# One order of work on five queues: gate, memory score and context row steps placed anew, and one query tile projected in plain fp32

## The reference, cut to what matters

```python
def memory_attention(q, mem_n, w_memkv):       # 4 heads of 64
    k, v = jnp.split(mem_n @ w_memkv, 2, axis=-1)
    s = jnp.einsum('bthd,bnhd->bhtn', q, k) * (MEM_HEAD_DIM ** -0.5)
    p = jax.nn.softmax(s, axis=-1)
    return jnp.einsum('bhtn,bnhd->bthd', p, v)

# first_block, per layer: q_mem and gate are columns of the same projection of h
branch = jnp.concatenate([mix, mem_o], axis=-1) * jax.nn.silu(gate)
x = x + branch @ w_out[i]
```

```python
def blk(qs):                                    # differential attention, 128 queries at a time
    s1 = jnp.einsum('bqhd,bkhd->bhqk', a, k1) * scale
    s2 = jnp.einsum('bqhd,bkhd->bhqk', b, k2) * scale
    w = jax.nn.softmax(s1, axis=-1) - lam * jax.nn.softmax(s2, axis=-1)
    return jnp.einsum('bhqk,bkhe->bqhe', w, v)

h  = _rms(x, g_pre) * (1.0 + scale) + shift
hc = _rms(xc, g_pre) * (1.0 + mod_c[1]) + mod_c[0]          # the context rows
y = jnp.concatenate([a_out * silu(na_g), b_out * silu(df_g), c_out * silu(cv_g)], -1) @ w_out
x_new = x + gate * _rms(y, g_post)
```

## Time and profile before

| | before |
|---|---|
| median of 3 runs | 1653.34 us (1653.30 to 1657.56) |
| the profiled execution | 1653.44 us |
| its span | 1651.6 us |
| PE busy | 1597.0 us, 97% of the span |
| DVE, ACT busy | 979.8 us (59%), 667.6 us (40%) |
| mean granted TensorE clock | 0.991 |

### The profile page before, as it was taken

How to read it: one execution, slowest core, us unless ns; L and a number is a source line. 1 busy time by engine, 2 the same in 40 slices (tenths; PEclk the granted TensorE clock), 3 DMA queues, 4 the chain that set the end, 5 groups by cost and what they waited for, 6 DMA issues and landing times.

```text
span 1651.6 us, 22948 instructions
## 1 busy us (share of the span) xinstructions
PE 1597.0 (97%) x8870; PEld 1277.7 (77%) x8870; DVE 979.8 (59%) x1803; ACT 667.6 (40%) x1323; POOL 140.7 (9%) x192
## 2 busy tenths in 40 slices
PE   7999999899999999999999999989999999999898
PEld 6977877687878878878888888865656887788676
DVE  1356454456556655665447787565665467876674
ACT  3365443424323323263313435244554325433653
POOL 4132100000000000002000110000112001000001
PEclk9999999899999999999999999999999999999899
DMA  8221244334654764462223111221003134213100
GB/s 289 81 77 50 103 153 117 80 82 121 190 158 120 155 185 139 148 151 68 92 96 109 56 54 40 92 93 58 1 26 96 48 107 140 58 39 128 52 14 39
DMA packets 171252, 161.36 MB, mean 98 GB/s; under 512 B 40374, under 2 KB 154280, under 8 KB 171112
## 3 DMA queue, kind: packets, MB, share of 16 engines
q1 hardware_dynamic: 151944, 126.97, 26.1%
q10 hardware_dynamic: 16928, 25.27, 4.7%
q0 software_dynamic: 2272, 7.64, 1.4%
HBM read 149.80 MB, written 11.18 MB: 97 GB/s over the span
## 4 chain that ended last, share of the span: by engine, by line
PE 83%; DVE 10%; ACT 4%; issue 2%; DMA 0%; POOL 0%; ACTq 0%; SPq 0%; POOLq 0%; DVEq 0%
PE psum L2596 46%; PE psum L2567 10%; PE psum L2630 7%; PE psum L3139 5%; PE psum L2621 4%; PE psum L3137 2%; PE psum L2775 2%; PE psum L2687 2%; PE psum L2730 2%; DVE arena L1999 1%; PE psum L2669 1%; PE psum L3010 1%; DVE arena L1969 1%; DVE wring_r L2076 1%; DVE arena L2133 1%
## 5 line engine op out<-in xcount | busy, mean ns | idle before, releaser
L2596 PE MATMUL psum<-hT_r,wring_r 128*128 128x512 f32 x1696 | 575.2, 393 | 3.6 <-ACT branch L1745 1.1
L2596 PEld LDWEIGHTS psum<-hT_r,wring_r 128*128 128x128 f32 x1696 | 319.3, 188 | 79.0 <-issue 10.0
L2596 PE MATMUL psum<-arena_r,wring_r 128*128 128x256 f32 (+1 forms) x1360 | 359.1, 333 | 0.7 <-ACT branch L1564 0.5
L1564 ACT ACTIVATE arena<-psum 128x512 f32<-128x512 f32 (+6 forms) x256 | 149.8, 611 | 416.0 <-PE psum L2596 244.2
L2596 PEld LDWEIGHTS psum<-arena_r,wring_r 128*128 128x128 f32 x1360 | 218.3, 190 | 26.2 <-issue 1.8
L2567 PE MATMUL psum<-arena 128*128 128x96 f32 (+9 forms) x1460 | 220.8, 365 | 16.9 <-ACT branch L1745 7.1
L2596 PE MATMUL psum<-arena_r 128*128 128x512 f32 (+1 forms) x720 | 224.5, 350 | 0.0
L2567 PEld LDWEIGHTS psum<-arena 128*128 128x128 f32 (+5 forms) x1460 | 160.8, 189 | 64.7 <-issue 31.9
L2596 PE MATMUL psum<-hT_r,arena_r 128*128 128x512 f32 x448 | 177.8, 397 | 1.8 <-DVE wring_r L2076 1.0
L2630 PE MATMUL psum<-ident,arena 128*128 128x128 f32 (+3 forms) x1104 | 145.9, 277 | 17.4 <-DMA arena<-in_c_ctx 7.4
L2630 PEld LDWEIGHTS psum<-ident,arena 128*128 128x128 f32 (+3 forms) x1104 | 125.2, 142 | 39.6 <-issue 14.6
(11 more groups left out here) (237 smaller groups left out, 1967.8 us busy)
## 6 DMA issues: line engine op xcount, KB each, us to landing
wring<-in_w_in_b SPq DMA_DIRECT2D x54, 512.0 KB, 5.9
arena<-in_w_mod ACTq DMA_DIRECT2D x16, 1536.0 KB, 8.3
wring<-in_w_in SPq DMA_DIRECT2D x16, 1536.0 KB, 6.9
wring<-in_w_out SPq DMA_DIRECT2D x8, 2048.0 KB, 8.4
wring<-in_w_in_a SPq DMA_DIRECT2D x5, 1536.0 KB, 6.6
arena<-x_dram SPq DMA_DIRECT2D x3, 2048.0 KB, 14.6
wring<-in_w_in SPq DMA_DIRECT2D x6, 1024.0 KB, 5.7
arena<-ebias_dram SPq DMA_DIRECT2D x144, 32.0 KB, 1.8
```

What stands on the lines that cost most here:

```text
L1564: return nc.scalar.activation(out, in_, ACT.Copy, scale=scale)
L2596: ins_ = nc.tensor.matmul(b[0:hi.shape[2], 0:width], w[:, k], v[:, k], start=k + p == 0, stop=(k, p) == (KT - 1, 2))
```

## The change

It does five things. In A, `mS` is cut in two steps of four banks, with `gate` 6 between them and `gate` 7 behind. In B, `gate` 4 goes ahead of `qm`, and `mS` follows `qm` directly. `hcT` of layer 1 moves from behind the last `doT` of layer 0 to a place ahead of `dPV` of the last but one item, so ahead of the last `dT` too. In layer 1, `nv` goes ahead of `nq`. And in layer 1's differential stage the first query tile is projected in plain fp32 (its own split steps go away), and the eight quarters of the output weights are split at items 8 to 11, two each, instead of items 4 to 8.

```diff
--- before.py
+++ after.py
@@ -36,7 +36,7 @@
-YO_SPLITS = {4: ((0, 0), (0, 1)), 5: ((0, 3),), 6: ((0, 2), (1, 0)), 7: ((1, 1), (1, 3)), 8: ((1, 2),)}
+YO_SPLITS = {8: ((0, 0), (0, 1)), 9: ((0, 3), (0, 2)), 10: ((1, 0), (1, 1)), 11: ((1, 3), (1, 2))}
@@ -169,9 +169,9 @@
     add("v" * 6, "AoT")
-    add("a" * 8, "mS", "A")
-    add("a", "gate", "A", 6)
-    add("a", "gate", "A", 7)
+    for part in range(2):
+        add("a" * 4, "mS", "A", part)
+        add("a", "gate", "A", 6 + part)
     add("av" * 4, "mT", "A")
@@ -198,11 +198,10 @@
-    for i in range(4):
+    for i in range(5):
         add("a", "gate", "B", i)
     add("av", "qm", "B")
-    add("a", "gate", "B", 4)
-    add("a" * 8, "mS", "B")
+    add("a" * 8, "mS", "B", 0)
     for g in range(2):
         add("aav", "Bproj", 0, g)
@@ -251,8 +250,11 @@
         add("av" * 3, "nvF", l)
-        add(lat_ctx * 3, "nq", l)
+        if l == 0:
+            add(lat_ctx * 3, "nq", l)
         add("aaaavv", "nv", l)
+        if l:
+            add(lat_ctx * 3, "nq", l)
         neighbourhood(add, l)
+def mem_jobs(key):
+
+    return range(8) if key[1] == "B" else range(4 * key[2], 4 * key[2] + 4)
@@ -497,7 +504,8 @@
-            rows = [(tiles[i - 1], 1)] if h == 1 and i else [(t, 0)] if n == 5 or (h == DH - 1 and i) else []
+            rows = [(tiles[i - 1], 1)] if h == 1 and i else [(t, 0)] if h == DH - 1 and i else []
+            rows = [row for row in rows if row[0] != tiles[0]]
@@ -523,9 +531,11 @@
             if todo:
                 project()
+            if n == len(items) and l == 0:
+                add("vvvv", "hcT", 1)
             if h == 0 and i:
                 add("v", "doT", l, tiles[i - 1])
-                if l:
+                if l and i > 1:
                     add("", "yb", tiles[i - 1], 1)
@@ -537,9 +547,7 @@
     add("v", "doT", l, last)
-    if l == 0:
-        add("vvvv", "hcT", 1)
-    else:
+    if l:
         add("", "yx", l, before)
...
@@ -2084,6 +2092,7 @@
                     dve.wait_ge(yo_w_hi, yo_ws.index((half, q)) + 1)
+                    read_by_pe(dve, ("yo", 1, 0, half, 1))
                     cut = slice(2 * q, 2 * q + 2)
...
@@ -3119,7 +3130,7 @@
                     if turned_last:
                         pe.wait_ge(last_hi, 1)
-                    elif l:
+                    elif l and t:
                         pe.wait_ge(yo_x_lo, yo_xs.index((t, piece)) + 1)
@@ -3128,14 +3139,14 @@
-                    for k in yo_rows(t, piece) if l and not turned_last else ():
+                    for k in yo_rows(t, piece) if l and t and not turned_last else ():
                         cut = slice(t * P, (t + 1) * P)
                         x_hi, x_lo, w_hi, w_lo = row_hi[t % 2][:, k], branch_r[:, k, cut], yo_hi[half][:, k], yo_lo[half][:, k]
-                        if t == 0:
+                        if t == 1:
                             pe.wait_ge(yo_w_lo, yo_ws.index((half, k // 2)) + 1)
                         for p, (v, m) in enumerate(((x_hi, w_hi), (x_lo, w_hi), (x_hi, w_lo))):
                             ins_ = nc.tensor.matmul(b, v, m, start=k + p == 0, stop=(k, p) == (5, 2))
-                    for k in yo_rows(t, piece) if l == 0 else ():
+                    for k in yo_rows(t, piece) if l == 0 or t == 0 else ():
                         ins_ = nc.tensor.matmul(b, src[:, k, tt * P:(tt + 1) * P], w[:, k], start=k == 0, stop=k == 5)
```

More of the change, by code:

```diff
@@ L932, in hybrid_stack_kernel @@
         before_mem = split_at[("Bproj", 1, 0), 0]
-        split_starts = [("wout", "A"), ("wout", "B"), ("hcT", 1)]
+        split_starts = [("wout", "A"), ("wout", "B"), ("doT", 0, TT - 1)]
         split_bounds = [sum(split_jobs(key) for key, _ in steps[:order_of[start]]) for start in split_starts]
@@ L1749, in _ @@
                     ph = "AB".index(key[1])
-                    for i in range(8):
-                        b = bank(key, i)
+                    for j_, i in enumerate(mem_jobs(key)):
+                        b = bank(key, j_)
                         act.wait_ge(mem_negmax, 8 * ph + i + 1)
@@ L2200, in _ @@
                     ph = "AB".index(key[1])
+                    jobs = mem_jobs(key)
                     def mem_normalise(i):
-                        evacuated(dve, key, i)
+                        evacuated(dve, key, i - jobs[0])
                         chained(nc.vector.reciprocal(m_rec[:, ph, i], m_sum[:, ph, i]))
@@ L2206, in mem_normalise @@
                             m_rec[:, ph, i].unsqueeze(2).to_broadcast([P, 2, NMEM])).then_inc(mem_probs, 1)
-                    for i in range(8):
-                        b = full(dve, key, i)
+                    for i in jobs:
+                        b = full(dve, key, i - jobs[0])
                         chained(nc.vector.reduce_max(m_max[:, ph, i], b[:, :].rearrange("p (h m) -> p h m", h=2), AX_X))
                         scaled(m_neg[:, ph, i], m_max[:, ph, i], -mem_scale).then_inc(mem_negmax, 1)
-                        if i:
+                        if i > jobs[0]:
                             mem_normalise(i - 1)
-                    mem_normalise(7)
+                    mem_normalise(jobs[-1])
                 elif kind == "mT":
@@ L2838, in _ @@
                     evacuated(pe, ("qm", ph), 1)
-                    for i in range(8):
+                    for i in mem_jobs(key):
                         t, odd = divmod(i, 2)
                         lo = odd * MD
-                        b = claim(pe, key, i)
+                        b = claim(pe, key, i - mem_jobs(key)[0])
                         for j in range(2):
```

## The result

| | before | changed |
|---|---|---|
| median, 19 runs of each | 1652.72 us (1649.82 to 1657.56) | 1657.70 us (1654.01 to 1659.82) |
| ratio | | 1.0027 [1.0021, 1.0034] |
| the profiled execution | 1653.44 us | 1654.35 us |
| its span | 1651.6 us | 1652.6 us |
| PE busy | 1597.0 us | 1595.3 us |

The change costs 0.27%, some 4.5 us; 1657.5 us was forecast. It was nearly its fastest run and shows only 0.9 us more than before's.

A forecast was written before the change was run, and what follows sets the result against it. PE, busy 97% of the span, was taken as the bound. Terms -9.9 (B), +0.9 (A), +11.5 (`hcT`), -0.9 (`nv`), +3.0 (plain fp32) sum to +4.6 us; forecast 1657.5 us, range 1650 to 1662.5.

The forecast's parts named there:

- Both signs: The forecast is wrong if the bracket at `dT` is under 5 us, or if B gives less than 8.
- B: Gate 4 ahead of `qm`: PE's waits of 7.08 and 0.84 us and half speed go, -9.9 us (-11.5 to -7).
- `hcT`: End of layer 0: DVE's eight pairs precede the combining, PE waits 7.8 us at `dT`: +11.5 us (+8 to +13).
- Nothing hides it: Within the `hcT` term: PE's list offers nothing else during the 7.8 us wait at the last `dT`.
- Scores in A: Scores in two halves: added table loads and a silu delay `mPV`, about +0.9 us.
- half speed in A too: Rival at `mPV` in A: half speed follows PE's early arrival, 1.7 us more, 1659.2 us; chance 0.07.
- `nv`: Layer 1, `nv` ahead of `nq`: waits of 0.97 and 0.48 us go, one of 0.6 comes, about -0.9 us.
- Plain fp32: Layer 1's first tile: +2.8 PE work, -4.0 at first `doT`, +4.2 at the second: +3.0 us (-1 to +5).

The follow-up runs named there:

- the experiment on `nv`: Gate 4 ahead of `qm` in B and `nv` ahead of `nq` in layer 1, against the kernel before: 1641.45 us, 0.9928 [0.9909, 0.9947].

## Why the prediction was right

The total was right, 1657.5 beside 1657.7, and partly by luck: two errors met. Both signs that the forecast named came out for it, a bracket at `dT` of 5 us or more (7.56) and at least 8 us from B.

The timed parts have intervals of some 2 us. The fourteen profiles price the parts more closely, by the time between the same two instructions of PE in each, here named by their times in the kernel before (us; in brackets the number of profiles; 1.7 us is taken off where a half-speed stretch of 3.41 us that belongs to `hcT` falls into the fourth):

| stretch | without the part | with it |
|---|---|---|
| A, 140.28 to 265.83 | 125.5 to 126.0 (9) | 126.8 to 127.1 (3), with half speed 129.5 and 130.0 |
| B, 265.83 to 721.26 | 454.9 to 455.5 (5) | 444.6 to 444.8 (8), 445.5 (1) |
| `hcT`, 1238.30 to 1278.56 | 40.3 (6) | 50.4 to 51.2 (5); one step later 44.8 to 45.1 (3) |
| `nv`, 1278.56 to 1518.52 | 240.0 to 240.8 (6) | 239.7 to 240.1 (6), 238.0 and 238.3 |
| plain fp32, 1546.78 to 1632.73 (`oN` behind the quarters) | 86.0 (5), 83.9 (1) | 86.9 (2), 87.2 (2), 88.4 (1) |

**B** forecast -9.9, measured -10.2, and -10.6 in the table. The piece was rounded by 304.42 and `qm` copied by 304.90 where 302.6 and 303.2 were forecast. Of these 1.8 and 1.7 us A's part explains 1, and it did no harm: the scores waited 0.99, not 0.9. All five profiled kernels with the wait of 7 us have 10.24 us at half speed beginning within it, at 310.5 to 315.6 us; none of the nine profiles without it has any there. That is as clear as such a link gets.

**`hcT`** forecast +11.5, measured +9.8 [7.6, 12.1]. The waits were 7.56 for 7.8 and 0.81 for 0.8. The clock was the term sized a little high: the profiles say 10.2 to 10.9 in all. The earlier trace rows gave 2.9, but at `dT` half speed covered more of the idle time: PE was busy in it for 3.67 to 5.06 us in the five profiles with this order, which is 1.8 to 2.5 us. "Nothing hides it" stands: all five profiles with this order have both the wait and the stretch.

**Scores in A** forecast +0.9, measured +4.1 [2.5, 6.0]. This is the step that failed. The waits themselves were sized nearly right, 1.2 us in the profiles where the clock stays up; that `mPV` starts 0.96 us later, as good as the 0.9 forecast, owes 0.3 to an early start. What was wrong is "half speed in A too", given 0.07 as a rival and left out of the term. The prediction gives no reason for so small a chance. Three waits, 0.42, 1.28 and 1.24, stand within 4 us there, and in two of five profiles half speed came with them, at 2.5 to 3 us each time. In before's profile one wait of 0.83 stands there and the other 15 us earlier, and half speed did not follow. Whether the clock falls here differs from execution to execution of one kernel with the same waits. The page "ScalarE: Activation LUTs", section "What ACT_TABLE_LOAD costs", of the Trainium skill would have come to +3.7, nearer to what was measured, but for a reason the rows deny. The silu and the exponential start 1.29 and 1.30 us after the start of their 1.28 us loads, and the second load starts 0.02 us after the silu ends, so there is no drain of 1.38, and the waits come to 1.2 or 1.3 us more, not 3.7.

**`nv`** forecast -0.9. The old waits, 0.97 and 0.48, went as said, and the new one ahead of `nv` is 0.63 as said (0.6). But 1.00 came at 1378.30, which nothing had foreseen. Set beside before's one profile nothing was gained (the neighbourhood scores start at 1395.08, before at 1395.09), but that profile is the shortest of the six without the part. The medians of the table's row are 240.6 without `nv` and 239.9 with it, so `nv` was worth about -0.7 us: the size was right, and the new wait took what the exchange gave beyond it. DVE's and POOL's rows show what the wait is:

```profile
1376.35 1.90 DVE L1980 TENSOR_SCALAR arena<-arena,stat 128x512 f32<-128x512 f32 x2
```

```profile
1376.45 1.51 POOL L1217 TENSOR_TENSOR arena<-arena,na_mask 128x512 f32<-128x512 f32 x1 [21.62 <-DMA arena<-ebias_dram]
```

The two scalings took 0.88 us in all before (at 1377.47), now 1.90: 0.49 and 1.50. The second coincides with an addition of POOL's that used to run at 1382.35 and now starts at 1376.45, as soon as its load lands. What lets that load land earlier is left open. The forecast looked at SP's queue for gate weights only, not for what POOL waits for. Six of the eight profiles with `nv` have this wait (0.95 to 1.07), with one of the two scalings at 1.47 to 1.59 us. In the other two (`hcT` one step later, and `oN` ahead, both in the changed kernel) POOL's addition starts just after the second scaling has: both scalings stay at 0.48 or 0.49, the addition takes 1.56 and 1.58 us instead of 1.26, PE has no such wait, and the stretch is shortest, 238.3 and 238.0. So the wait comes of that meeting, and a few tenths of a us in when POOL's load lands decide on 1.5 to 1.9 us. The rival of the experiment on `nv`, that the waits are only exchanged, is not borne out by the profiles; the times cannot tell.

**Plain fp32** forecast +3.0, measured +2.3 [0.8, 3.6]. The first wait went, 2.39 came (2.35 to 2.6 forecast). DVE did not fall behind, as argued. The table's row depends on the clock near 1547 us: where it stayed up, the stretch is 86.9 with the part (twice; 88.4 once, with twice as much half speed at the second `doT`) and 83.9 without it (once), 2.9 more, which is the +3.0 forecast.

So with the measured sizes, and `nv` from the profiles: -10.2 + 4.1 + 9.8 - 0.7 + 2.3 = +5.3, beside 4.5 [3.5, 5.6] for the whole and 4.6 forecast. The forecast had A 3.2 us too low, and `hcT`, plain fp32 and B 1.7, 0.7 and 0.3 too high. Had the chance of half speed in A been priced higher alone, the total would have been worse.

What the first profile of the changed kernel seems to say, +0.9, is in part the execution. By the same stretches it is +1.3 (A), -10.6 (B), +10.2 (`hcT`), -0.1 (`nv`), +0.9 (layer 1's differential stage) and -0.7 elsewhere. The clock took little in it: no half speed at `mPV` (2.5 to 3 us where it comes), at `dT` 0.5 to 0.8 us less than in the four other profiles with this order, and none at 1547 us in layer 1, where nine of the fourteen profiles have 6.83 us or more. That last stretch is worth 2.0 us, by the kernel with `hcT` moved, which lacks it (83.9 beside 86.0). It does not come evenly: six of the seven profiles without plain fp32 have it, three of the seven with it. Whether that part shares in it is not shown.

## What to carry to other kernels

Where an in-order list feeds five queues, cost a moved step by its longest share on any queue, and ask of each thing behind it, not only the next, who waits for it: `hcT` cost 9.8 us ahead of the combining and still 6.9 behind it, since the eight pairs then held the addition behind. Price a wait together with half speed behind it, and where short waits come close together, as three within 4 us did here, give that more than a small chance (two of five profiles here). And with a clock that differs between executions of one kernel, read from one profile where a wait is, and from timed parts, or from the same stretch in many profiles, what it is worth. One profile of before made `nv` look worth nothing.

## What the runs showed of the hardware

**VectorE and GpSimd held each other up.** A scaling of 128x512 on DVE took 1.50 us instead of 0.48 while POOL's 1.51 us addition ran from 0.3 us before it. The Trainium skill's page "SBUF — State Buffer", section "Who interferes with whom", says that such a scaling can use the port pair that the two engines share, and that whoever comes first keeps it for the whole instruction; this trace agrees, the later one starting 0.3 us behind and ending 0.3 us after POOL's. In the two profiles where the scaling started first, by 0.06 and 0.08 us, it took 0.48 us and POOL's addition 1.58 and 1.56 instead of 1.26. Where the two started within 0.01 us of each other, the scaling was held (1.59).

**Half speed after long and after short waits.** With the waits of 7 us or more it came every time, beginning within the wait (five of five in B, five of five at `dT`). With shorter ones it differs from place to place: at the first `doT` (2.3 us) in five of five profiles (in a sixth it had come 7 us ahead of the `doT`, which then waited only 1.43 us), at the second (2.4 us) in three of five, at `mPV` in two of five. And short waits, too, can go with it every time: all fourteen profiles have 6.83 us of it near 1100 us, in layer 0's differential stage, beside waits of up to 1.3 us. The single runs of the changed kernel spread from 1654.0 to 1659.8 us, with mean clocks of 0.993 to 0.990.

**Half speed costs half of the time that PE is busy in it, not half of its length.** At `mPV` PE was busy for 5.67 us of a stretch of 6.83, and it cost 2.8 us (6.48 beside 3.70). The nine stretches of 10.24 us in B and at `dT` began within waits of 7 us, and PE was busy for 4.65 to 6.22 us of them, which is 2.3 to 3.1 us of time. It costs less still where a wait behind it shrinks: 2.0 us near 1547 us, with PE busy in all 6.83.
